# Output, gate, up and down products: high and low activations as one 512-column moving operand, halves added as the tile leaves PSUM

## The reference, cut to what matters

```python
mixed = g[:, :, 0] * o_a + g[:, :, 1] * o_b + g[:, :, 2] * o_c
x = x + mixed @ w_out                                     # 1024 x 1024
h2 = _rms(x) * norm2_g
x = x + (jax.nn.silu(h2 @ w_ffn_gate) * (h2 @ w_ffn_up)) @ w_ffn_down   # 1024 x 2816, 2816 x 1024
```

## Time and profile before

| | us |
|---|---|
| median of 3 runs | 2523.76 (2520.39 to 2523.99) |
| the profiled execution | 2515.88 |
| its span, first to last instruction | 2514.1 |
| PE busy | 2000.3 (80%), 12744 matmuls |
| PE weight loads busy | 1402.5 (56%) |
| DVE busy | 843.5 (34%) |
| ACT busy | 444.0 (18%) |
| POOL busy | 346.2 (14%) |

### The profile page before, as it was taken

One profiled execution on the slowest core, in us unless ns is written; L12 is line 12 of the kernel. 1 busy time (PEld: TensorE's weight loads), 2 busy tenths in 40 slices (PEclk: granted clock), 3 DMA queues, 4 the chain that ended last, 5 costly groups with the idle time before them and its releaser, 6 DMA issues.

```text
span 2514.1 us, 29575 instructions
## 1 busy us (share of the span) xinstructions
PE 2000.3 (80%) x12744; PEld 1402.5 (56%) x12744; DVE 843.5 (34%) x1186; ACT 444.0 (18%) x429; POOL 346.2 (14%) x75
## 2 busy tenths in 40 slices
PE   6999998999999998999899777656556565556565
PEld 6987778999998777999757564111111111111111
DVE  6854338435756326635336442000000000000001
ACT  3522002334432111332131102000000000000000
POOL 3400013555510002554000000000000000000000
PEclk9999889999999989999999887787787878887877
DMA  6433434656433432566421016999999999999996
GB/s 227 160 134 112 157 126 135 208 161 194 168 134 134 169 146 80 168 191 162 162 101 68 17 69 268 417 417 417 417 418 418 417 418 417 418 417 418 417 417 260
DMA packets 230873, 613.01 MB, mean 244 GB/s; under 512 B 11196, under 2 KB 106684, under 8 KB 197180
## 3 DMA queue, kind: packets, MB, share of 16 engines
q1 hardware_dynamic: 228704, 602.19, 63.0%
q10 hardware_dynamic: 2076, 9.45, 1.0%
HBM read 610.55 MB, written 1.05 MB: 243 GB/s over the span
## 4 chain that ended last, share of the span: by engine, by line
PE 54%; DMA 23%; SPq 11%; DVE 8%; ACT 2%; issue 2%; POOL 0%; ACTq 0%; DVEq 0%; PEldq 0%
SPq L1159 11%; PE PS L1278 10%; DMA work<-in_w_up 8%; DMA work<-in_w_gate 7%; PE PS L1336 7%; PE PS L1330 7%; PE PS L1331 7%; DMA work<-in_w_down 7%; PE PS L559 5%; PE PS L741 2%; PE PS L1260 1%; PE PS L755 1%; DVE hT L2219 1%; DMA ring<-in_w_in 1%; PE PS L1496 1%
## 5 line engine op out<-in xcount | busy, mean ns | idle before, releaser
L741 PE MATMUL PS<-ring,proj 128*32 128x512 f32 x1280 | 194.7, 741 | 125.3 <-DMA ring<-in_w_up 68.5
L1211 POOL TENSOR_TENSOR ring_low<-ring,high_f 128x2048 fp32r<-128x2048 f32 (+1 forms) x42 | 228.5, 5440 | 258.6 <-ACT high_f L1715 258.6
L755 PE MATMUL PS<-work,proj 128*32 128x512 f32 x768 | 132.1, 823 | 105.8 <-DMA work<-in_w_down 105.8
L741 PE MATMUL PS<-work,proj 128*32 128x512 f32 x768 | 130.3, 814 | 101.9 <-DMA work<-in_w_up 65.9
L1278 PE MATMUL PS<-hT,ring 128*128 128x256 f32 x896 | 198.6, 380 | 0.0
L1121 DVE TENSOR_TENSOR proj<-proj,PS 128x512 f32<-128x512 f32 x16 | 11.0, 687 | 545.2 <-PE PS L741 545.2
L1330 PE MATMUL PS<-xh_f,high_f 128*128 128x256 f32 x768 | 184.3, 280 | 5.4 <-DVE hT_low L1910 5.4
L741 PEld LDWEIGHTS PS<-ring,proj 128*32 128x32 f32 x1280 | 38.7, 124 | 267.5 <-DMA ring<-in_w_up 110.4
L1331 PE MATMUL PS<-xh_f,ring_low 128*128 128x256 f32 x768 | 183.8, 278 | 0.0
L1278 PEld LDWEIGHTS PS<-hT,ring 128*128 128x128 f32 x896 | 168.3, 190 | 24.3 <-issue 1.7
L1715 ACT ACTIVATE high_f<-ring 128x4096 fp32r<-128x4096 f32 (+1 forms) x42 | 135.4, 3223 | 262.6 <-PE PS L1336 207.8
(11 more groups left out here) (418 smaller groups left out, 3289.8 us busy)
## 6 DMA issues: line engine op xcount, KB each, us to landing
ring<-in_w_gate SPq DMA_DIRECT2D x96, 1024.0 KB, 19.6
work<-in_w_down SPq DMA_DIRECT2D x96, 1024.0 KB, 19.6
ring<-in_w_in SPq DMA_DIRECT2D x74, 1024.0 KB, 7.3
work<-in_w_up SPq DMA_DIRECT2D x64, 1024.0 KB, 25.2
ring<-in_w_up SPq DMA_DIRECT2D x64, 1024.0 KB, 25.0
work<-in_w_gate SPq DMA_DIRECT2D x32, 1024.0 KB, 23.5
ring<-in_w_down SPq DMA_DIRECT2D x32, 1024.0 KB, 25.3
ring<-in_w_ada SPq DMA_DIRECT2D x24, 1024.0 KB, 6.9
```

The costliest lines, as they stand in the source:

```text
L741: mm = nt.matmul(PS[32 * j:32 * j + 32, 2 + n // 4, :], XSE[:, k, :], w[:, F_E * kk + 512 * j:F_E * kk + 512 * (j + 1)], start=(k == 0), s ...
L755: mm = nt.matmul(PS[32 * g:32 * g + 32, 5, :], HTE[:, P * c + 32 * d:P * c + 32 * (d + 1)], w[:, D * c + 512 * dh:D * c + 512 * (dh + 1)], ...
L1211: pool.tensor_tensor(ring_low[:, n % RING, c], w, high(n)[:, c].bitcast(F32), ALU.subtract).then_inc(low_pool, 1)
```

## The change

`wide_product` stands beside `split_product`. For each k one matmul of 512 columns takes the high weights over x_low and x_high at once (`XF` and `HIDS` are laid out so that both are one access pattern), into a bank of its own for each feature block (banks 4 to 7): one half of the bank holds w_high x_low, the other w_high x_high. The matmuls with the low weights, 256 columns, add into the half that x_high uses. All but the last of the 512-column ones come first, and only then does PE wait for the low weights. The engine that empties the tile has to add the two halves: `residual` adds them to xT in two instructions; in gate and up ACT copies one half to SBUF and DVE adds the other, silu works on the SBUF copy, and the product of silu and up is an instruction of its own with both inputs in SBUF. `BY_ACT` no longer holds any block of this stage. Blocks marked in `WIDE` are made so: the four of the output product, gate and up from the fourth block on, and down from the second. `hT_low` moves out of hT and is called `XL_F`.

```diff
--- before.py
+++ after.py
@@ -90,7 +90,10 @@
     SLOT_DONE[S_DOWN + _n] = Q_DOWN + _n + 1
 
 UNSCALED = 3
-BY_ACT = [UNSCALED <= q < N_PROJ or (Q_FFN < q < Q_DOWN and (q - Q_FFN) % 2 == 0) for q in range(LAYER_BLOCKS)]
+BY_ACT = [UNSCALED <= q < N_PROJ for q in range(LAYER_BLOCKS)]
+
+
+WIDE = [Q_OUT <= q < Q_FFN or Q_FFN + 3 <= q < Q_DOWN or q > Q_DOWN for q in range(LAYER_BLOCKS)]
 
 
 def taken_at(l, q):
@@ -331,8 +334,10 @@
 
 
         XH_A, XL_A = rounded("xh_a", "work", 9216, [KD, T]), rounded("xl_a", "work", 11264, [KD, T])
-        XH_F, hT_low = rounded("xh_f", "work", 3072, [KD, T]), rounded("hT_low", "hT", 0, [KD, T])
-        HID_H, HID_low = rounded("hid_h", "proj", 28 * T, [FB, T]), rounded("hid_low", "proj", 0, [FB, T])
+        XF = rounded("xf", "work", 1024, [2, KD, T])
+        XH_F, XL_F = XF[:, 0, :, :], XF[:, 1, :, :]
+        HIDS = rounded("hids", "proj", 0, [2, 28, T])
+        HID_low, HID_H = HIDS[:, 0, 0:FB, :], HIDS[:, 1, 0:FB, :]
 
         def width(n):
 
@@ -382,6 +387,16 @@
 
         def bank(l, q):
             return (LAYER_BLOCKS * l + q) % 2
+
+        def silu_at(l, n, step):
+
+            per = [[g and WIDE[Q_FFN + 2 * g], True, g > 0] for g in range(N_FFN // 2)]
+            return sum(map(sum, per)) * l + sum(map(sum, per[:n])) + sum(per[n][:step + 1])
+
+        def halves(l, q, n):
+
+            v = PS[:, 4 + 2 * bank(l, q):4 + 2 * bank(l, q) + n, :]
+            return v[:, :, 0:T], v[:, :, T:2 * T]
 
         def full(l, n):
             return 32 * (LAYER_SLOTS // RING * l + n // RING + 1)
@@ -1336,6 +1351,29 @@
                         mm = nt.matmul(out, h[:, c:c + P], low_x[:, k, :], start=False, stop=(k == kn - 1))
                 mm.then_inc(block_done, 1)
 
+            def wide_product(l, q, n, weight, pair, high_x, kn, n_blocks=2):
+
+                j = SPLIT.index(n)
+                pe.wait_ge(high_ready, len(SPLIT) * l + j + 1)
+                taken(l, q)
+                h, w = high(n), ring_low[:, n % RING, :]
+                at = 0 if high_x is XH_F else T
+                for b in range(n_blocks):
+                    both = PS[:, 4 + 2 * bank(l, q) + b, :]
+                    for k in range(kn - 1):
+                        c = weight(b, k)
+                        nt.matmul(both.rearrange("p (a t) -> p a t", t=T), h[:, c:c + P], pair[:, :, k, :], start=(k == 0), stop=False)
+                    if b == 0:
+                        pe.wait_ge(low_dve, len(SPLIT) * l + j + 1)
+                        if j:
+                            pe.wait_ge(low_pool, (len(SPLIT) - 1) * l + j)
+                    for k in range(kn):
+                        c = weight(b, k)
+                        nt.matmul(both[:, at:at + T], w[:, c:c + P], high_x[:, k, :], start=False, stop=False)
+                    c = weight(b, kn - 1)
+                    mm = nt.matmul(both.rearrange("p (a t) -> p a t", t=T), h[:, c:c + P], pair[:, :, kn - 1, :], start=False, stop=True)
+                mm.then_inc(block_done, 1)
+
             def norm_sums(m, lo, hi):
 
                 for k in range(lo, hi):
@@ -1636,7 +1674,7 @@
                 pe.wait_ge(h_ready, 7 * l + 3)
                 for n in range(2):
                     for i in range(2):
-                        split_product(l, Q_OUT + 2 * n + i, S_OUT + n, lambda b, k: 512 * k + P * (2 * i + b), XH_F, hT_low, KD)
+                        wide_product(l, Q_OUT + 2 * n + i, S_OUT + n, lambda b, k: 512 * k + P * (2 * i + b), XF, XH_F, KD)
 
             def ffn(l):
                 for n in range(N_FFN // 2):
@@ -1649,10 +1687,12 @@
                         else:
                             if n == 1 and g == 0:
                                 pe.wait_ge(h_ready, 7 * l + 4)
-                            split_product(l, q, S_FFN + n, w, XH_F, hT_low, KD, low_at=7 * l + 5 if n == 1 and g == 0 else None)
-                for n in range(N_DOWN):
-                    split_product(l, Q_DOWN + n, S_DOWN + n, lambda b, k: P * k, HID_H, HID_low, FB, 1,
-                                  last_at=7 * l + 6 if n == 0 else None, low_at=7 * l + 7 if n == 0 else None)
+                                split_product(l, q, S_FFN + n, w, XH_F, XL_F, KD, low_at=7 * l + 5)
+                            else:
+                                wide_product(l, q, S_FFN + n, w, XF, XH_F, KD)
+                split_product(l, Q_DOWN, S_DOWN, lambda b, k: P * k, HID_H, HID_low, FB, 1, last_at=7 * l + 6, low_at=7 * l + 7)
+                for n in range(1, N_DOWN):
+                    wide_product(l, Q_DOWN + n, S_DOWN + n, lambda b, k: P * k, HIDS, HID_H, FB, 1)
 
             pe.sem_inc(block_done, START)
             for l in range(LAYERS):
@@ -1808,14 +1848,15 @@
             def ffn(l):
 
                 for n in range(N_FFN // 2):
-                    if n == 0:
-                        act.wait_ge(dve_taken, taken_at(l, Q_FFN))
-                        na.activation(SILU[:, 0, :], SILU[:, 0, :], ACT.Silu).then_inc(silu_ready, 1)
-                    else:
+                    silu = SILU[:, n % 2, :]
+                    if WIDE[Q_FFN + 2 * n]:
                         act.wait_ge(block_done, done(l, Q_FFN + 2 * n))
-                        if n >= 2:
-                            act.wait_ge(dve_taken, taken_at(l, Q_FFN + 2 * n - 3))
-                        na.activation(SILU[:, n % 2, :], PS[:, bank(l, Q_FFN), :], ACT.Silu).then_inc(act_taken, 1)
+                        na.activation(silu.rearrange("p (a b) -> p a b", b=T), halves(l, Q_FFN + 2 * n, 2)[0], ACT.Copy).then_inc(silu_ready, 1)
+                    act.wait_ge(dve_taken, taken_at(l, Q_FFN + 2 * n))
+                    na.activation(silu, silu, ACT.Silu).then_inc(silu_ready, 1)
+                    if n:
+                        act.wait_ge(block_done, done(l, Q_FFN + 2 * n + 1))
+                        na.activation(HID[:, 2 * n:2 * n + 2, :], halves(l, Q_FFN + 2 * n + 1, 2)[0], ACT.Copy).then_inc(silu_ready, 1)
                     high_weights(l, S_FFN + 2 + n)
                     if n == 1 and l + 1 < LAYERS:
                         act.wait_ge(h_ready, 7 * l + 4)
@@ -2233,7 +2274,12 @@
                 for i in range(n):
                     dve.wait_ge(block_done, done(l, q0 + i))
                     x = xT[:, blocks * i:blocks * (i + 1), :]
-                    nv.tensor_tensor(x, x, banks(bank(l, q0 + i), 1, blocks, T), ALU.add).then_inc(dve_taken, 1)
+                    if WIDE[q0 + i]:
+                        first, second = halves(l, q0 + i, blocks)
+                        link(nv.tensor_tensor(x, x, first, ALU.add))
+                        nv.tensor_tensor(x, x, second, ALU.add).then_inc(dve_taken, 1)
+                    else:
+                        nv.tensor_tensor(x, x, banks(bank(l, q0 + i), 1, blocks, T), ALU.add).then_inc(dve_taken, 1)
                     dve.wait_ge(dve_taken, taken_at(l, q0 + i))
                     if gain is not None:
                         for k in range(blocks * i, blocks * (i + 1)):
@@ -2249,16 +2295,23 @@
                 for n in range(N_FFN // 2):
                     x, h = HID[:, 2 * n:2 * n + 2, :], HID_H[:, 2 * n:2 * n + 2, :]
                     silu = SILU[:, n % 2, :].rearrange("p (a b) -> p a b", b=T)
-                    dve.wait_ge(block_done, done(l, Q_FFN + 2 * n + 1))
-                    if n == 0:
-                        nv.tensor_tensor(x, banks(bank(l, Q_FFN + 1), 1, 2, T), rstd_wide, ALU.mult).then_inc(dve_taken, 1)
-                        dve.wait_ge(dve_taken, taken_at(l, Q_FFN + 1))
-                        dve.wait_ge(silu_ready, l + 1)
-                        link(nv.tensor_tensor(x, x, silu, ALU.mult))
+                    gate, up = Q_FFN + 2 * n, Q_FFN + 2 * n + 1
+                    if n:
+                        dve.wait_ge(block_done, done(l, gate))
+                        if WIDE[gate]:
+                            dve.wait_ge(silu_ready, silu_at(l, n, 0))
+                            nv.tensor_tensor(silu, silu, halves(l, gate, 2)[1], ALU.add).then_inc(dve_taken, 1)
+                        else:
+                            nv.tensor_copy(silu, banks(bank(l, gate), 1, 2, T)).then_inc(dve_taken, 1)
+                    dve.wait_ge(block_done, done(l, up))
+                    if n:
+                        dve.wait_ge(silu_ready, silu_at(l, n, 2))
+                        nv.tensor_tensor(x, x, halves(l, up, 2)[1], ALU.add).then_inc(dve_taken, 1)
                     else:
-                        dve.wait_ge(act_taken, taken_at(l, Q_FFN + 2 * n))
-                        nv.tensor_tensor(x, banks(bank(l, Q_FFN + 1), 1, 2, T), silu, ALU.mult).then_inc(dve_taken, 1)
-                        dve.wait_ge(dve_taken, taken_at(l, Q_FFN + 2 * n + 1))
+                        nv.tensor_tensor(x, banks(bank(l, up), 1, 2, T), rstd_wide, ALU.mult).then_inc(dve_taken, 1)
+                    dve.wait_ge(dve_taken, taken_at(l, up))
+                    dve.wait_ge(silu_ready, silu_at(l, n, 1))
```

(5 more changed lines are left out.)

## The result

| | before | after |
|---|---|---|
| median, us | 2520.85 (10 runs) | 2530.18 (10 runs) |
| lowest to highest | 2518.8 to 2523.99 | 2523.6 to 2534.28 |
| ratio, 95% interval | | 1.0033 [1.0021, 1.0044] |
| profiled execution, its span | 2515.88, 2514.1 | 2531.87, 2530.1 |

The account below looks back on a forecast made before the run. PE was taken to bound the feed-forward part. Seam, gate and up, down and layer-end terms gave -1.15 us in layer 0 and -1.65 in layer 1, -2.8 in all: 2521.0 us, range 2511 to 2531 (own range 2517 to 2525).

Parts of the forecast that it names:

- What bounds the stage: Feed-forward part: PE itself is the bound, busy 80.00 of 80 us, so a removed matmul is worth its spacing.
- The matmuls: All wide products: one 512-column matmul costs 226.8 ns against 234.4 for two narrow, saving 7.6 ns for each of 1044 removals.
- rival 3: Wide matmuls cost as much as two narrow ones beside DMA, ACT and DVE traffic: 6.9 us lost, 2528; chance 0.12.
- Output product: Four output blocks save 0.49 us, but second adds delay DVE, so POOL starts first at the second feed-forward slot.
- The step that failed: Second feed-forward slot: POOL takes 4.52 us, then DVE's low half 2.2; XH_F comes late, +2.4 us a layer.
- rival 5: Second feed-forward slot: POOL also holds the XU low parts; XH_F 1.9 us later still, +3.8 in all, 2525; chance 0.10.
- Down: Seven wide down blocks: -1.2 us a layer, plus half the excess over clean blocks; -1.7 and -2.3 us by layer.
- Rival 4: Gate and up: POOL gets ahead of DVE in every pair, PE waits 0.8 us each, 14 us, 2535; chance 0.08.
- Signs asked for: Spacing near 227 ns, pair 11.0 us; POOL first, DVE's half over 5, PE idle 2 before XH_F; down blocks 7.6.
- gate and up: -2.2 booked for each: Gate and up: 19 wide blocks at 0.12 us give -2.3 a layer, with +0.1 charged in the first pair.
- the layer ends: Last residual of each layer: one more add on the way to PE or the norm, +0.35 and +0.45 us.

Follow-up runs that it names:

- x4: Kernel before, same matmuls reordered: in every split product all high weights on x_high first, then all low weights; 2524.25 us, ratio 1.0022.
- e1: The changed kernel with the four output blocks of each layer narrow again, gate, up and down still wide; 2515.9 us, ratio 0.9976.
- x3: Kernel before, all products narrow, plus one VectorE copy of the last output block's PSUM tile ahead of its add; 2532.86 us, ratio 1.0047.
- e4: The changed kernel plus one wait: POOL's half of the second feed-forward slot's low weights starts after DVE's half; 2516.22 us, ratio 0.9984.
- e2: Kernel before with only the four output blocks of each layer made wide; 2533.35 us, ratio 1.0039.
- y1: e1 with the two feature blocks of a gate and up tile interleaved for each k; 2512.24 us, ratio 0.9965.
- x1: e4 with the activations' high and low parts side by side, so the 512-column operand is contiguous; 2520.25 us, ratio 1.0000.

## Why the prediction was wrong, step by step

- **What bounds the stage**: right for gate and up. PE is busy 80.00 of 80 us after as before.
- **The matmuls**: the term was mis-sized. 230 + 120 ns for a wide and a narrow one stand against 226.8 + 117.2; a removal saves 1.7 ns, and gate and up give 0.25 us a layer, not 2.2. The values were taken from rows with another order: 117.2 belongs to alternating high and low weights, and the change gives that order up. Against the same matmuls in runs (x4) merging saves 6.6 ns, so the value of the merge was about right, and what the sum had at nothing was the price of the new order, 4.8 ns a removal as far as x4's narrow matmuls can stand for the new kernel's. The rule of the Trainium skill ("TensorE: Matmul & The Clock Gate", Back-to-back issue gap), which I set aside because the spacings lay above it, lets two merged matmuls save one fixed part, 2.5 ns. As a number this is nearer to the net 1.7, but the 6.6 of the comparison in runs is above it, so these traces do not bear the rule out. In its size the result is nearly rival 3, which gave the whole saving away; its reason, the company of other engines, is not what x4 shows.
- **Output product**: DVE late, POOL first: right, in both layers (430.05 and 1027.05, each within 0.1 us of the end of ACT's high part, as worked out). The saving was 0.10 to 0.12 instead of 0.49. The 1.4 us more in layer 0 is clock at the start of the product (granted 0.60 from 402.19 to 406.00); in e1, whose output product is narrow, the same falls on layer 1 (0.50 from 995 to 997), and x4, with no wide product at all, has it in both layers (27.19 and 26.18 us for the stretch at a granted 0.89 and 0.93), so it is not the wide product's.
- **The step that failed**: "takes 4.52 alone, and DVE's half then needs 2.2" and "Price: +2.4 us a layer at that point". The held instruction was not DVE's half of the low weights (2.28 us, free) but the one before, the second of the XU low parts (5.12 us for the two instead of 0.87), on which PE waits directly: PE idled 3.53 us, and the row grew by 5.95 and 5.94 us, not 2.4. The prediction's own times had said so: with DVE ready for its half at 427.85, the two XU low parts run from 426.98, and POOL begins at 427.07, inside them. That is rival 5, which I gave 0.10 because eight scalar_tensor_tensor at 433.62 took 3.60 us with POOL's record still open. That row did not speak against the lock, as a free row beside it shows: the eight take 3.25 when POOL is idle (442.32 in the kernel after). A query by line of the kernel before, window 430 to 437, has the minimum, median and maximum of one in ns:

```profile
L1938 DVE SCALAR_TENSOR_TENSOR hT<-xT,par,work x8: 471/473/822, 433.6 to 436.7; 128x256 f32<-128x256 f32 x8
```

The first of the eight was held by 0.35, until about 433.97. POOL's record runs to 434.16, and in after and x3 too the release, reckoned back from the end of the held instruction, lies 0.2 us before the end of POOL's record. So the end of a POOL record is not the moment at which DVE goes on, and two records that overlap do not show that the instructions ran together. And the same line at 34.93 of the kernel before had eight of them in 5.22 us beside POOL, the longest 2445 ns:

```profile
34.93 5.22 DVE L1938 SCALAR_TENSOR_TENSOR hT<-xT,par,work 128x256 f32<-128x256 f32 x8
```

The evidence was in the trace; I had read one instance. The rule of the Trainium skill ("SBUF — State Buffer", Who interferes with whom), that a VectorE instruction with two SBUF inputs contends with a GpSimd one that reads SBUF, holds for this form: 5.12 against 0.87.
- **Rival 5's price**: 2.4 + 1.9 = 4.3 us a layer at this point; measured 5.94 less 0.1 of the output product, 5.8 (layer 1). I had XH_F late by DVE's chain and left out what PE's idle time does to its clock, 1.7 us a layer.
- **Down**: the sum is right, -1.5 and -2.8 against -1.7 and -2.3, and so is the sign asked for, seven blocks at 7.66 us with no waits. The two terms of the sum are both off and make up for each other, which is luck: against a clean block of 7.74 a wide one saves 0.08 us, 0.6 a layer and not 1.2, and the excess over clean went nearly whole, 0.9 and 2.2, where I had booked half.
- **Rival 4** (POOL first in every pair) did not come: DVE stays first in gate and up, pair 11.20. POOL comes first by 0.1 us only at the first two down slots (552.05 and 563.25 against 552.15 and 563.36), where PE shows no idle time behind it.
- **Signs asked for**: spacing 230 (inside the 232 allowed, pair off), POOL first (right), PE idle before the first block on XH_F (wrong place: it idled before XU_L), DVE's half over 5 us (wrong: 2.28), no wait inside the pairs (right but for the 0.16 us at 459.04).

From the forecast to what the cut of the traces shows, both layers together:

| | us |
|---|---|
| forecast | -2.8 |
| output product and unscaled blocks: +2.4 booked for each layer, +7.23 and +5.84 measured | +8.3 |
| gate and up: -2.2 booked for each, -0.27 and -0.25 measured | +3.9 |
| down: -1.7 and -2.3 booked, -1.51 and -2.79 measured | -0.3 |
| the layer ends, booked at +0.8, lie outside the cut | -0.8 |
| sum | +8.25 |

Without the held XU low parts (e4) the form pays, 0.9984, and without the wide output product (e1) 0.9976.

## What to carry to other kernels

When two engines exclude each other, work out who is first from the start times in microseconds, and then which instruction the other engine starts next: that one is the victim (here the second of two short ones), not the one that you were looking at. An order that holds by 0.05 us should be written as a wait (e4) before anything is added in front of it. Take the spacing of an instruction from a row in the order that the new kernel will have. Never size a held or free duration from one row; ask for the minimum and maximum of the same line.

## What the runs showed of the hardware

- A VectorE scalar_tensor_tensor with both tensors in SBUF is held by a GpSimd tensor_tensor for as long as that runs: 5.12 us for 0.87 (after, e2), 5.13 (x3). One that was running when GpSimd began was not held (480 ns), the next one was (4722 in after, 4731 in x3).
- The release of the held instruction lies 0.2 us before the end of GpSimd's record (before at 433.62, after, x3).
- PE idle for 3.5 us was followed in after and x3 (layer 0) by a granted clock of 0.66 and 0.67 over 5 us, and in e2 by 0.83 over the whole 20.6 us of the row; the same matmuls without the idle time ran at 1.00 (e1).
- The same 96 matmuls of a gate and up pair take 11.255 us with high and low weights alternating on one slice, 11.41 in runs (x4). Which property of the order it is stays open: the moving operand alone (y1) explains 1.4 ns of a wide one and nothing of a narrow one. Compared in runs, two 256-column matmuls merged to one of 512 save 6.6 ns (11.41 against 11.20 us a pair).
- A moving operand of two 256-column segments 8 KB apart costs the same in gate and up as 512 adjacent columns (112.91 us a layer in e4 and x1).
